# Attention of a two-layer block: un-normalised weights are transposed, 1/sum goes in with the gate, rotary products come before the turn

## The chip, the cores and the metric

The kernel runs on one core of a Trainium2 chip. The metric is the device time of one execution in microseconds, as the median of several runs. A profile of one execution gives the rows that are shown here. Engines in the rows: PE is TensorE (matmul), PEld its weight loads, DVE VectorE, ACT ScalarE, POOL GpSimd, SP the engine that issues the weight transfers.

## The reference

The reference is a long chain on one sequence of 256 positions, width 1024, in 32-bit floats: a first block (four mixers and a SwiGLU layer, then the mixers and a mixture of experts), and a second block of two layers. The change is in the second block.

- Even layer: a state-space scan beside a dilated attention. 24 heads of 64 in three groups of windows; queries and keys are normalised per head and get a partial rotary embedding; the three groups are merged by a softmax over their log-sums, so for one query the 512 weights of three groups are one softmax. The result is multiplied by silu(g), joined with the scan's output and projected.
- Odd layer: attention with 16 heads of 64. With 256 positions there is one block of keys, so it is causal softmax attention. Queries and keys are normalised and rotated the same way, the result is multiplied by silu(g) and projected:

```
q = partial_rope(rms_norm(q, q_norm), pos);  k = partial_rope(rms_norm(k, k_norm), pos)
p = softmax(masked(q @ k.T * scale));        o = (p @ v) * silu(g);        x = x + o @ w_out
```

## The kernel before

Features lie on partitions, positions along the free dimension (T = 256). Weights stream from HBM in pieces of up to 1 MB into a ring of six slots. ScalarE rounds each piece to a high part (`rounds`), VectorE or GpSimd subtracts to a low part (`rests`, `rest_piece`, L501), and TensorE takes each projection as three matmuls per tile (`mm3`). These matmuls, the bulk, fill most of the program. A matmul on full 32-bit floats (`mm`, L383) shows as two instructions in the trace.

Each engine runs its own program in a fixed order, written by hand: a string of letters (`EVEN`, `ODD`) that `walk` goes through, the same on every engine. A `.` is a step of the bulk (in these stretches half a piece, 24 matmuls), `Q` a step of the rotary turn, `A` of the attention, `R` of its reciprocals, `O` of the output projection, `D` of the scan, `Y` of splitting its output. Semaphores join the engines. The core of the odd layer is five times `AQRQ.`; that of the even one is `AQRQ` twice and `AQRQQ` twice, without bulk.

The rotary turn works on tiles of 128 features (two heads) by 256 positions, 24 in the even layer and 16 in the odd. It is x cos + (P x) sin, with a permutation P of features within a head (constant `pp`). The even layer's tiles come as three of queries, then three of keys; the odd layer's in turn. Step s on the engines:

- TensorE, `turn_pe`: for a key tile it spreads that tile's normalising factors over a bank ("key factors", eight instructions), then multiplies tile s - 1 by P into a bank of its own ("turn"), which must have been read for tile s - 2.
- VectorE, `turn_dve`: scales tile s ("unturned"; L399 for keys, L402 for queries), reads the turned tile s - 1 times sin (L2377, "sin part"), adds the cosine part (L2380, "turned").
- GpSimd, `turn_pool`: the tile times cos (L2391, "cos part"), and at three steps the low part of a weight piece.

The attention takes cases of two heads: eight in the even layer (128 queries by 512 keys and groups), eight in the odd (two query blocks, 384 columns). Three cases are under way at a time; in step t:

- TensorE, `attend_pe`: scores of case t; weights of case t - 1 turned so that keys lie on partitions, a matmul of each 128 by 128 block with a diagonal of 1/sum; values of case t - 2.
- VectorE, `attend_dve`: scales and masks the scores (L399), takes their bound (L2456), multiplies the values of case t - 2 by half the gate ("attended"), and in `R` takes the reciprocal of the sums (L2473).
- ScalarE, `attend_act`: the exponential with its sum (L411), the copy of the turned weights out of PSUM ("weights by key", L408), and in `R` the diagonals, identity times 1/sum (L408).

VectorE evacuates the scores of case t ahead of everything else in that step, since its queue is in order.

## Time and profile before

| | |
|---|---|
| median of 3 runs | 1939.07 us (1939.01 to 1939.71) |
| span of the profiled execution | 1942.9 us; the profile has no other time of it |
| PE busy | 1882.1 us, 97% |
| DVE busy | 1310.0 us, 67% |
| ACT busy | 943.8 us, 49% |
| POOL busy | 124.2 us, 6% |
| mean granted TensorE clock | 0.993 |

Matmuls are pipelined and their ends are modelled, so busy time of PE counts also what overlaps. A wait is put down to the engine and line whose semaphore came last. The granted clock is a share of 2.4 GHz.

### The profile page before, as it was taken

What the parts mean: (1) busy time and instruction counts of PE and PEld (TensorE: products, weight loads), DVE (VectorE), ACT (ScalarE), POOL (GpSimd) and SP (SyncE); (2) the same over time, 40 slices, a digit from 0 to 9 for tenths busy, and PEclk for the clock granted to TensorE, in tenths of its full rate; (3) what the DMA queues carried; (4) which work ended last, traced back from release to release, by engine and by line L of the source; (5) the groups of instructions that cost most, each with busy time, mean ns of one, the idle gap of its engine ahead of it and who ended that gap; (6) DMA issues with size and microseconds to landing.
All of it is one profiled execution on the core that took longest, in us unless ns stands there. A gap on an engine that the chain in (4) does not pass through costs nothing.

```text
span 1942.9 us, 34150 instructions
## 1 busy us (share of the span) xinstructions
PE 1882.1 (97%) x14477; PEld 1737.7 (89%) x14477; DVE 1310.0 (67%) x1864; ACT 943.8 (49%) x1150; POOL 124.2 (6%) x82
## 2 busy tenths in 40 slices
PE   9999999999999999999999999999999999889998
PEld 9889999999988999998888888888899989789978
DVE  7975566654599647665556668989888456856563
ACT  5353345434444423444435457767756453445453
POOL 0000000000000000000100011010200001100034
PEclk9999999999999999999999999999999999999999
DMA  8221246455542223544545568999945333314320
GB/s 309 88 88 56 100 165 224 163 185 184 182 140 88 72 63 134 197 171 158 182 153 194 182 229 312 331 328 335 334 180 173 131 109 119 111 54 164 131 88 23
DMA packets 52679, 321.84 MB, mean 166 GB/s; under 512 B 6320, under 2 KB 9648, under 8 KB 19760
## 3 DMA queue, kind: packets, MB, share of 16 engines
q1 hardware_dynamic: 52096, 317.76, 46.5%
q8 instruction: 115, 1.88, 0.4%
q10 hardware_dynamic: 432, 1.90, 0.3%
q14 instruction: 36, 0.29, 0.1%
HBM read 317.01 MB, written 1.05 MB: 164 GB/s over the span
## 4 chain that ended last, share of the span: by engine, by line
PE 78%; DVE 14%; ACT 4%; issue 3%; POOL 0%; DVEq 0%; ACTq 0%; POOLq 0%
PE b L383 77%; DVE s_arena L399 5%; DVE s_ring_lo L501 3%; ACT s_wh L408 2%; PE b L2055 1%; DVE s_arena L1433 1%; DVE s_arena L2456 1%; DVE s_arena L402 0%; ACT s_arena L408 0%; ACT s_arena L405 0%; DVE s_arena L637 0%; DVE s_arena L2377 0%; DVE s_roots L399 0%; ACT s_arena L411 0%; POOL s_ring_lo L501 0%
## 5 line engine op out<-in xcount | busy, mean ns | idle before, releaser
L501 DVE TENSOR_TENSOR s_ring_lo<-s_ring,s_wh 128x2048 fp32r<-128x2048 f32 (+3 forms) x310 | 648.1, 2096 | 309.3 <-ACT s_wh L408 308.7
L408 ACT ACTIVATE s_wh<-s_ring 128x2048 fp32r<-128x2048 f32 (+3 forms) x332 | 574.1, 1732 | 253.2 <-PE b L383 249.2
L383 PE MATMUL b<-s_Hh,s_wh 128*128 128x256 f32 x1832 | 536.2, 293 | 9.2 <-DVE s_arena_r L2983 4.2
L383 PE MATMUL b<-s_Hl,s_wh 128*128 128x256 f32 x1832 | 521.6, 285 | 0.0
L383 PE MATMUL b<-s_Hh,s_ring_lo 128*128 128x256 f32 x1832 | 521.4, 285 | 0.0
L383 PEld LDWEIGHTS b<-s_Hh,s_wh 128*128 128x128 f32 x1832 | 354.5, 194 | 20.0 <-issue 10.2
L383 PEld LDWEIGHTS b<-s_Hl,s_wh 128*128 128x128 f32 x1832 | 354.8, 194 | 0.5
L383 PEld LDWEIGHTS b<-s_Hh,s_ring_lo 128*128 128x128 f32 x1832 | 354.4, 193 | 0.0
L383 PE MATMUL b<-s_wh,s_arena_r 128*128 128x512 f32 (+1 forms) x942 | 296.4, 384 | 4.5 <-DVE s_arena_r L2294 3.7
L383 PE MATMUL b<-s_arena_r,s_wh 128*128 128x256 f32 x1184 | 214.6, 282 | 4.7 <-DVE s_arena L399 1.7
L383 PEld LDWEIGHTS b<-s_wh,s_arena_r 128*128 128x128 f32 x942 | 176.0, 188 | 38.9 <-DVE s_arena_r L2294 4.9
L383 PE MATMUL b<-s_arena 64*64 64x64 f32 (+7 forms) x2440 | 196.8, 260 | 11.5 <-ACT s_arena L408 3.6
L383 PEld LDWEIGHTS b<-s_arena 64*64 64x64 f32 (+3 forms) x2440 | 157.8, 149 | 42.0 <-issue 6.1
L408 ACT ACTIVATE s_arena<-b 128x256 f32<-128x256 f32 (+6 forms) x185 | 82.9, 476 | 229.4 <-PE b L383 204.1
L383 PEld LDWEIGHTS b<-s_arena_r,s_wh 128*128 128x128 f32 x1184 | 181.9, 188 | 7.0 <-DVE s_arena L399 3.1
L383 PE MATMUL b<-s_ring_lo,s_arena_r 128*128 128x512 f32 (+1 forms) x482 | 183.7, 381 | 0.0
L383 PE MATMUL b<-s_wh,s_Hh 128*128 128x256 f32 (+2 forms) x512 | 176.6, 345 | 0.0
L383 PE MATMUL b<-s_ring_lo,s_Hh 128*128 128x256 f32 (+2 forms) x512 | 170.4, 333 | 0.0
L383 PE MATMUL b<-s_arena_r,s_ring_lo 128*128 128x256 f32 x592 | 166.4, 281 | 0.0
L383 PE MATMUL b<-s_wh,s_Hl 128*128 128x256 f32 (+2 forms) x464 | 152.4, 329 | 0.0
L501 POOL TENSOR_TENSOR s_ring_lo<-s_ring,s_wh 128x1536 fp32r<-128x1536 f32 (+1 forms) x22 | 85.6, 3892 | 747.9 <-ACT s_wh L408 747.7
L383 PEld LDWEIGHTS b<-s_arena_r,s_ring_lo 128*128 128x128 f32 x592 | 111.3, 188 | 0.0
(195 smaller groups left out, 1925.1 us busy)
## 6 DMA issues: line engine op xcount, KB each, us to landing
s_ring<-fixed SPq DMA_DIRECT2D x158, 1024.0 KB, 4.9
s_ring<-experts SPq DMA_DIRECT2D x96, 1024.0 KB, 5.0
s_ring<-experts SPq DMA_DIRECT2D x48, 768.0 KB, 4.4
s_ring<-fixed SPq DMA_DIRECT2D x24, 256.0 KB, 4.1
s_c<-c SPq DMA_DIRECT2D x1, 1664.0 KB, 17.6
s_ring<-fixed SPq DMA_DIRECT2D x3, 512.0 KB, 5.9
s_arena<-s_arena SPq DMA_DIRECT2D x48, 32.0 KB, 1.9
s_c<-c ACTq DMA_DIRECT2D x1, 1344.0 KB, 6.1
```

What stands on the lines that cost most here:

```text
L383: return e.matmul(out, l, r, start=start, stop=True, skip_group_check=True)
L399: return e.scalar_tensor_tensor(out=out, in0=a, scalar=s, in1=b, op0=o0, op1=o1)
L408: return e.activation(out, x, ACT.Copy, scale=scale)
L501: e.tensor_tensor(l_, r_, h_.bitcast(F), SUB).then_inc(*up(engine, z % "lo", i))
L1433: e.tensor_tensor(Gm[o:o + 64, q // 2, 2 * h2:2 * h2 + 2, :], (b7, b6)[n % 2][o:o + 64, :].rearrange("p (a n) -> p a n", a=2), rwm, MUL).t ...
L2055: last = e.transpose(b[:, 128 * j:128 * j + n], m_vb[t % 2][0:n, 128 * j:128 * j + 128], ident[0:n, 0:n])
L2456: last = e.tensor_reduce(m[:, 0, hh, k:k + 1], v[:, at:at + n], AX.X, MIN)
```

## The change

In `turn_dve` the products with cos and sin are formed before TensorE's turn, on VectorE: for a query tile two instructions straight from the raw tile, for a key tile the scaled tile and then two products. TensorE turns the product with sin (the two halves that P exchanges have the same sin), and VectorE adds the turned tile, straight from PSUM, to the product with cos. The turn of a tile now waits until the tile before it has been added ("turned"). `turn_pool` is gone; GpSimd keeps the low parts of the late weight pieces in the odd layer.

In the attention the un-normalised weights are transposed (`e.transpose`, one instruction each) instead of multiplied with a diagonal, and the diagonals on ScalarE are gone. Before the values of a case TensorE spreads 1/sum over the free half of the bank, with one matmul per head and sum. VectorE first multiplies the gate by half of that and then the values by the result, two instructions that depend on each other.

```diff
@@ -2354,54 +2354,43 @@
                     spread(e, banks2[0], r, [tiles[s][0]]).then_inc(*up("PE", "key factors", name, s))
                 if s:
                     if s >= 2:
-                        e.wait_ge(*on("sin part", name, s - 2))
+                        e.wait_ge(*on("turned", name, s - 2))
                     mm(e, banks2[1][:, 0:T], c("pp"), tmps[s - 1][2], True).then_inc(*up("PE", "turn", name, s - 1))
...
         def turn_dve(e, name, tiles, banks2, tmps, raw):
+            cos, sin = {"even": (c("cpe"), c("spe")), "odd": (c("cp"), c("sp"))}[name]
             for s in range(len(tiles) + 1):
                 if s < len(tiles):
                     j, key, is_k = tiles[s]
-                    un = tmps[s][2]
+                    own, un, across = tmps[s]
                     if s >= 2:
-                        e.wait_ge(*on("turn", name, s - 2))
-                        e.wait_ge(*on("cos part", name, s - 2))
+                        e.wait_ge(*on("turned", name, s - 2))
                     if is_k:
                         e.wait_ge(*on("key factors", name, s))
-                        stt(e, un, raw[:, j, :], pc(key), banks2[0][:, 0:T], MUL, MUL).then_inc(*up("V", "unturned", name, s))
+                        stt(e, un, raw[:, j, :], pc(key), banks2[0][:, 0:T], MUL, MUL).then_inc(*up("V"))
+                        e.wait_ge(*now("V"))
+                        e.tensor_tensor(across, un, sin, MUL).then_inc(*up("V", "unturned", name, s))
+                        e.tensor_tensor(own, un, cos, MUL).then_inc(*up("V", "own part", name, s))
                     else:
-                        ts(e, un, raw[:, j, :], pc(key), None, MUL).then_inc(*up("V", "unturned", name, s))
+                        stt(e, across, raw[:, j, :], pc(key), sin, MUL, MUL).then_inc(*up("V", "unturned", name, s))
+                        stt(e, own, raw[:, j, :], pc(key), cos, MUL, MUL).then_inc(*up("V", "own part", name, s))
                 if s:
-                    tmp, tm2, un = tmps[s - 1]
                     e.wait_ge(*on("turn", name, s - 1))
-                    e.tensor_tensor(tm2, banks2[1][:, 0:T], c({"even": "spe", "odd": "sp"}[name]), MUL).then_inc(*up("V", "sin part", name, s - 1))
-                    e.wait_ge(*on("cos part", name, s - 1))
-                    e.wait_ge(*now("V"))
-                    e.tensor_tensor(raw[:, tiles[s - 1][0], :], tmp, tm2, ADD).then_inc(*up("V", "turned", name, s - 1))
-                yield
-
-        def turn_pool(e, name, tiles, tmps, pieces={}):
-            for s in range(len(tiles) + 1):
-                if s:
-                    tmp, tm2, un = tmps[s - 1]
-                    if s >= 3:
-                        e.wait_ge(*on("turned", name, s - 3))
-                    e.wait_ge(*on("unturned", name, s - 1))
-                    pool_free(e)
-                    e.tensor_tensor(tmp, un, c({"even": "cpe", "odd": "cp"}[name]), MUL).then_inc(*up("G", "cos part", name, s - 1))
-                if s in pieces:
-                    rest_piece(e, pieces[s], "G")
+                    e.wait_ge(*on("own part", name, s - 1))
+                    e.tensor_tensor(raw[:, tiles[s - 1][0], :], banks2[1][:, 0:T], tmps[s - 1][0], ADD).then_inc(*up("V", "turned", name, s - 1))
+                yield
...
@@ -2420,10 +2409,9 @@
                 if 1 <= t <= len(cases):
                     case = cases[t - 1]
                     for hh in range(2):
-                        e.wait_ge(*on("diagonal", name, t - 1, hh))
-                        for j, k in enumerate(case.blocks):
-                            last = mm(e, case.banks[hh][:, 128 * j:128 * j + 128], z.v[(t - 1) % 2][hh][:, 128 * j:128 * j + 128],
-                                      z.d[(t - 1) % 2][hh][k], True)
+                        e.wait_ge(*on("weights", name, t - 1, hh))
+                        for j in range(len(case.blocks)):
+                            last = e.transpose(case.banks[hh][:, 128 * j:128 * j + 128], z.v[(t - 1) % 2][hh][:, 128 * j:128 * j + 128], ident)
                         last.then_inc(*up("PE", "weights turned", name, t - 1, hh))
...
                     for hh in range(2):
                         e.wait_ge(*on("weights by key", name, t - 2, hh))
+                        e.wait_ge(*on("one over sum", name, t - 2, hh))
+                    for k in range(len(case.sums)):
+                        for hh in range(2):
+                            mm(e, case.banks[0][HALVES[hh], 256 + 128 * k:384 + 128 * k],
+                               z.m[t % 2][:, 2, hh, k:k + 1].broadcast_to([128, 64]), ident, True)
                     for n, (val, at, w_, to) in enumerate(case.vals):
                         for hh in range(2):
                             last = mm(e, case.banks[0][HALVES[hh], to:to + w_], val(hh), z.t[t % 2][hh][:, at:at + w_], n == 0)
...
                 if t >= 2:
                     case = cases[t - 2]
-                    o = case.banks[0][:, 0:max(to + w_ for _, _, w_, to in case.vals)]
+                    width = 128 * len(case.sums)
+                    o, over = case.banks[0][:, 0:width], case.banks[0][:, 256:256 + width]
+                    if case.gate.shape != o.shape:
+                        o, over = (z_.rearrange("p (a m) -> p a m", a=2) for z_ in (o, over))
+                    e.wait_ge(*on("out", li["og", (t - 2) // 2] if name == "oo" else li["eg", (t - 2) // 4]))
                     e.wait_ge(*on("values", name, t - 2))
-                    if case.gate.shape != o.shape:
-                        o = o.rearrange("p (a m) -> p a m", a=2)
-                    e.wait_ge(*on("out", li["og", (t - 2) // 2] if name == "oo" else li["eg", (t - 2) // 4]))
-                    stt(e, case.out, o, 0.5, case.gate, MUL, MUL).then_inc(*up("V", "attended", name, t - 2))
+                    stt(e, case.gate, over, 0.5, case.gate, MUL, MUL).then_inc(*up("V"))
+                    e.wait_ge(*now("V"))
+                    e.tensor_tensor(case.out, o, case.gate, MUL).then_inc(*up("V", "attended", name, t - 2))
...
                 if t < len(cases):
                     yield
-                    for hh in range(2):
-                        e.wait_ge(*on("one over sum", name, t, hh))
-                        if t >= 2:
-                            e.wait_ge(*on("weights turned", name, t - 2, hh))
-                        for k in range(len(cases[t].sums)):
-                            last = copy(e, z.d[t % 2][hh][k], ident, scale=z.m[t % 2][:, 2, hh, k:k + 1])
-                            last.then_inc(*(up("A", "diagonal", name, t, hh) if k == len(cases[t].sums) - 1 else up("A")))
...
                 last.then_inc(*(up("G", "tap pads") if z is e_pad[1] else up("G")))
-            e.wait_ge(c2_in, 16)
-            turn_pool(e, "even", e_tiles, e_tmps)
...
         def odd_pool(e):
-            turn_pool(e, "odd", o_tiles, o_tmps, {9: odd_late[0], 11: odd_late[1], 15: odd_late[2]})
-            for p in odd_late[3:]:
+            for p in odd_late:
                 rest_piece(e, p, "G")
```

## Rows read from the trace of the kernel before

**Rows 1.** Page, part 4: the chain that ended last, by engine.

```profile
PE 78%; DVE 14%; ACT 4%; issue 3%; POOL 0%; DVEq 0%; ACTq 0%; POOLq 0%
```

**Rows 2.** Window, length, busy PE, PEld, DVE, ACT, POOL (instructions); granted clock; DMA.

```profile
1664.00:1720.00 56.00, 45.63 (x406) 37.55 (x405) 49.04 (x123) 25.75 (x59) 8.71 (x12) 0.97 0.17 60
1862.00:1907.00 45.00, 39.90 (x330) 33.27 (x329) 31.51 (x89) 27.61 (x78) 20.47 (x12) 1.00 0.14 48
```

**Rows 3.** PE, two odd cycles: start, length, instructions [idle before <-releaser].

```profile
1871.88 3.26 PE L383 MATMUL b<-s_arena 64*128 64x128 f32 x28
1874.97 0.61 PE L383 MATMUL b<-s_c,s_roots 128*64 128x128 f32 x8
1875.50 0.70 PE L383 MATMUL b<-s_arena,s_c 128*128 128x256 f32 x2
1876.81 0.67 PE L383 MATMUL b<-s_arena,s_c 128*128 128x256 f32 x2 [0.61 <-DVE s_arena L2377]
...
1880.28 3.26 PE L383 MATMUL b<-s_arena 64*128 64x128 f32 x28
...
1886.10 0.67 PE L383 MATMUL b<-s_arena,s_c 128*128 128x256 f32 x2 [1.50 <-DVE s_arena L2377]
```

**Rows 4.** Timeline of DVE in the first of these cycles.

```profile
1875.45 0.42 DVE L399 SCALAR_TENSOR_TENSOR s_arena<-b,s_arena 128x256 f32<-128x256 f32 x1
1875.79 0.47 DVE L399 SCALAR_TENSOR_TENSOR s_arena<-s_arena,s_par,b 128x256 f32<-128x256 f32 x1
1876.24 0.42 DVE L2377 TENSOR_TENSOR s_arena<-b,s_c 128x256 f32<-128x256 f32 x1
1876.77 0.62 DVE L2380 TENSOR_TENSOR s_arena<-s_arena 128x256 f32<-128x256 f32 x1
```

**Rows 5.** Timeline of PE in an even cycle.

```profile
1690.88 0.67 PE L383 MATMUL b<-s_arena,s_c 128*128 128x256 f32 x2 [0.70 <-DVE s_arena L2377]
1693.11 4.16 PE L383 MATMUL b<-s_arena 64*128 64x256 f32 x44 [1.56 <-DVE s_arena L2380]
```

**Rows 6.** Timeline of DVE in the same even cycle.

```profile
1689.64 0.38 DVE L399 SCALAR_TENSOR_TENSOR s_arena<-b,s_arena 128x128 f32<-128x128 f32 x1
1689.92 0.47 DVE L399 SCALAR_TENSOR_TENSOR s_arena<-s_arena,s_par,b 128x256 f32<-128x256 f32 x1
...
1691.59 0.33 DVE L402 TENSOR_SCALAR s_arena<-s_arena,s_par 128x256 f32<-128x256 f32 x1
```

**Rows 7.** Timelines of PE: transposes, and weights turned by diagonals.

```profile
1514.19 0.64 PE L2725 MATMUL b<-s_c,s_arena 128*128 128x128 f32 x4
...
1672.58 2.05 PE L383 MATMUL b<-s_arena 128*128 128x128 f32 x16 [1.27 <-ACT s_arena L408]
```

**Rows 8.** L2380 (min, median, max); L399 with two SBUF inputs (count, busy, mean).

```profile
L2380 DVE TENSOR_TENSOR s_arena<-s_arena x40: 425/700/727, 1624.6 to 1905.0; 128x256 f32<-128x256 f32 x40
...
L399 DVE SCALAR_TENSOR_TENSOR s_arena<-s_arena 128x256 f32<-128x256 f32 x56 | 24.5, 475 | 2.1 <-ACT s_arena L2918 1.3
```

**Rows 9.** Timeline of PE at an earlier pair of rotary turns.

```profile
1844.79 0.67 PE L383 MATMUL b<-s_arena,s_c 128*128 128x256 f32 x2 [0.61 <-DVE s_arena L2377]
```

**Rows 10.** Timeline of PE at the last even cases.

```profile
1716.71 7.14 PE L383 MATMUL b<-s_arena 64*128 64x256 f32 x44 [2.36 <-ACT s_arena L408]
```

**Rows 11.** Short stretches, columns as in rows 2.

```profile
1688.80:1692.20 3.40, 2.04 (x18) 1.09 (x14) 3.26 (x10) 2.48 (x8) 0.87 (x2) 1.00 0.00 0
1712.70:1716.10 3.40, 1.65 (x22) 1.29 (x20) 3.05 (x9) 2.14 (x6) 0.00 (x0) 1.00 0.00 0
1716.10:1719.50 3.40, 2.79 (x15) 2.49 (x16) 1.37 (x4) 1.56 (x4) 0.00 (x0) 0.53 0.00 0
1784.30:1787.70 3.40, 3.40 (x30) 3.40 (x30) 2.29 (x2) 1.19 (x1) 0.00 (x0) 1.00 0.72 289
1791.10:1794.50 3.40, 3.40 (x18) 3.40 (x19) 1.75 (x1) 3.31 (x5) 0.00 (x0) 0.54 0.50 212
```

**Rows 12.** Timeline of POOL in the odd layer.

```profile
1870.41 4.64 POOL L501 TENSOR_TENSOR s_ring_lo<-s_ring,s_wh 128x2048 fp32r<-128x2048 f32 x1
```

More of the change, by code:

```diff
@@ L2399, in build @@
         Case = namedtuple("Case", "after banks parts sums blocks vals out gate part")
-        Buffers = namedtuple("Buffers", "v t d m")
+        Buffers = namedtuple("Buffers", "v t m")
         def attend_buffers(ar, n, groups):
             return Buffers([[ar(n) for _ in range(2)] for _ in range(2)], [[ar(n) for _ in range(2)] for _ in range(2)],
-                           [[[ar(128) for _ in range(groups)] for _ in range(2)] for _ in range(2)], [ar(3, 2, groups) for _ in range(2)])
+                           [ar(3, 2, groups) for _ in range(2)])
```

## The prediction

> **What bounds the kernel now.** I began with the chain of work that ended last: 78% of it is TensorE matmul, 14% VectorE [rows 1]. That is an average over a long program, so I went on to the busy time by stretch, for the two places the change touches: the even attention (1664 to 1720 us) and the odd one (1862 to 1907 us) [rows 2]. The reader is to see that they differ. In the even stretch VectorE is busy 49.0 of 56.0 us and TensorE 45.6: VectorE sets the pace. In the odd one TensorE is busy 39.9 of 45.0 us and VectorE 31.5: neither is full, so a few waits from one to the other cost 5 us.
>
> The order of TensorE's instructions shows where [rows 3]. An odd cycle is: the scores of a case, the weights turned (case before), the values (two before), key factors, a rotary turn, **a wait for L2377**, a second rotary turn, 24 projection matmuls, the next scores. The wait is 0.61 us in one cycle and 1.50 in the next. VectorE's order of the same moment [rows 4] shows what it waits for: after the scores VectorE evacuates them, gates the case two before (L399, 1875.45), multiplies out the next tile, and only then does the sine part (L2377) that frees the bank of the turn. The path is thus TensorE's scores, VectorE's whole row of work up to that release, TensorE's second turn, the projection. What stands between scores and second turn on TensorE itself is covered. The even cycle has the same form, with waits of 0.70 and 1.56 us [rows 5, 6].
>
> **The change on TensorE: less work, mostly not on the path.** A turned weight block is today a matmul with a diagonal, two instructions; 16 such instructions take 2.05 us. Four transposes elsewhere in the trace take 0.64 us [rows 7]. Both rows hold the full length of their last instruction; between them lie 12 instructions and 1.41 us, so 0.12 us each, if both kinds have one pace. A block then costs one instruction of 0.12 us and not two. The even layer has 8 cases of 8 blocks, the odd 8 of 6: 112 x 0.12 = -13.4 us. The matmuls that spread 1/sum are 4 instructions per even case and 8 per odd one; key factors, the same shape, take 0.61 us for 8 [rows 3], of which about 0.17 lies under what follows: 8 x 0.22 + 8 x 0.44 = +5.3 us. Net -8.1 us of TensorE time. Bounds for a transpose: 0.64 / 4 = 0.16 us, and no gain at all would be the 0.24 us of the pair it replaces. The Trainium skill (TensorE: Matmul & The Clock Gate, Terms) calls the transpose mode four times faster for FP32; the rows say twice, and by the page's figure some 6 us more would go, most of it from time that is covered.
>
> **The change on ScalarE and GpSimd.** 48 diagonal copies go (16 even cases' halves, 32 odd), and 40 cosine parts. Nothing on the path waits for them except the first even case (1.27 us, `ACT L408` [rows 7]); it is counted below. VectorE's adds (L2380) lose an odd delay: they take 700 ns by the median and 425 at least [rows 8], as most start while GpSimd's cosine part runs. The Trainium skill (SBUF — State Buffer, SBUF: two separate sides) says that GpSimd and a VectorE instruction with two SBUF inputs lock each other out; the two numbers agree with it.
>
> **The change on VectorE: this sets the time.** Steps are from start to start, since instructions overlap by some 0.08 us; a result that the next instruction needs costs a wait of 0.11 us instead (1876.24 + 0.42 to 1876.77) [rows 4].
> - Gating becomes two dependent instructions. Odd: today 0.34 us (1875.45 to 1875.79); after 0.42 + 0.11 + 0.34 = 0.87, **+0.53**. Even: today 0.28 (1689.64 to 1689.92) [rows 6]; after 0.38 + 0.11 + 0.28, **+0.48**.
> - Key tile, from its start to the release of the bank. Today 0.47 (with overlap 0.40) and 0.42: 0.82 us. After: 0.47 + 0.11, two multiplications of 0.34, the add 0.42 = 1.68, as the turn now waits for "turned" and both products stand ahead of that add in VectorE's queue: **+0.86**. Where VectorE today waits for the turn itself (0.45 instead of 0.40) [rows 4], +0.81.
> - Where VectorE is full, a tile counts in all. Query tile: today 0.25 (0.33 less the overlap [rows 6]) + 0.53 + 0.62 (0.70 less the overlap) = 1.40 us; after, two instructions with two SBUF inputs, 475 ns each [rows 8] less the overlap, and the add, 0.39 + 0.39 + 0.34 = 1.12: **-0.28**. Key tile: 0.40 + 0.53 + 0.62 = 1.55 today, 0.58 + 3 x 0.34 = 1.60 after, +0.05.
>
> Odd layer. Five cycles: three with the long wait +1.39, two with the short one +1.34: +6.9 us. Two earlier pairs of turns, the later at 1844.8 with a wait of 0.61 us [rows 9], get +0.85 each: +1.7. What TensorE saves inside the cycles only lengthens its wait. Outside them one case's transposes run in the open, -0.7, of which a later wait may eat half: -0.4. The last two transposed cases save 1.4 us, three spreads take 1.4 back. Sum **+8.2 us**.
>
> Even layer. Ahead of case 2 two query tiles shorten VectorE's row: -0.5. Cases 2 and 3: two gatings +0.96, three key tiles +0.15, one query tile -0.28: +0.8. Cases 4 and 5: two gatings +0.96, two query tiles -0.5, two key tiles +0.1, and the last pair, where the products delay the turn's release by 0.87 but the separate sine part goes (-0.53 behind it): +0.9. After case 6 TensorE waits 2.36 us for ScalarE's copies [rows 10]; that chain is unchanged. Behind it TensorE is the bound: eight instructions fewer in each of two cases, at 0.24 us each in the first, which runs at the lower clock (44 matmuls in 7.14 us [rows 10], against 4.16 [rows 5]), -1.9, and -1.0 in the second; three spreads +0.8; the later gating before the output projection +0.5: -1.6. Sum **-0.4 us**.
>
> **TensorE's clock.** Rows of it are clear, the effect is not. From 1712.7 to 1716.1 us TensorE was busy 1.65 of 3.40 us, and in the stretch behind it the granted clock was 0.53, the lower level, 1.2 GHz; from 1688.8, busy 2.04 of 3.40, it stayed at 2.4 GHz [rows 11]. In the changed kernel the wait before the second turn grows, by VectorE's delay and TensorE's own saving (0.3 us), from 0.61 to 2.2 us and from 1.50 to 3.1 in the odd cycles, from 0.70 to about 2.8 in the even ones. These are as long as the 2.36 us ahead of that fall. A price: at the lower clock 18 matmuls ran in 3.40 us, at the full one 30 [rows 11]; 12 x 0.12 = 1.4 us lost. Bounds: no fall, 0; one in each of the five odd cycles twice as long as this row, 14 us. I take three or four more stretches of 3.4 us than before, **+5 us**, by the nearest row, the wait of 2.36 us.
>
> Sum: 8.2 - 0.4 + 5 = +12.8 us. It is made against the profiled span of 1942.9 us, which lies 3.8 us above the median of the runs; 1939.1 + 12.8 = **1951.9 us**.
>
> **Rivals.** 0.2% of this kernel is 3.9 us, about what a measurement can tell from no change.
> - *The path grows, the clock stays.* Same steps, no more time at 1.2 GHz. For it: waits of 1.50 and 1.56 us left the clock alone. 1939.1 + 7.8 = 1946.9 us. Chance 0.20.
> - *The clock falls in nearly every cycle.* In this kernel it would do so if transposes counted for less than the matmuls that they replace: 7.8 + 14 = +21.8, 1960.9 us. The trace has four transposes at a time among matmuls, never a dozen beside a wait, so it speaks neither way. Chance 0.08. The Trainium skill (TensorE: Matmul & The Clock Gate, PE-mode transpose) says that transposes don't count as busy for the clock in the same way; no row here shows it.
> - *Other side: TensorE is the bound after all.* If VectorE had slack enough to release the bank before TensorE came to the second turn, TensorE's -8.1 us would all count: 1931 us. It decides if VectorE could release the bank 1.4 us sooner than it does; both waits in [rows 3] end at VectorE, against it. Chance 0.06.
> - *Nothing shows.* VectorE's additions and TensorE's savings cancel, because my delay of the release is half as large: within 3.9 us of 1939.1. Chance 0.06.
> - *GpSimd's splits of weights in the way.* They take 4.6 us each [rows 12], and nothing ties them to the rotary steps any more. A product with two SBUF inputs that starts under one would be held up as the adds are under the cosine parts [rows 8], here by up to 4.6 us, half of it for a typical hit: with one or two hits 1954 to 1957. The splits follow ScalarE's roundings, which end ahead of VectorE's evacuation of scores from PSUM, against it. Chance 0.05.
>
> My own case has 0.55, with its own range 1948 to 1960. Sum of the slower cases 0.55 + 0.20 + 0.08 + 0.05 = 0.88; faster 0.06; same 0.06. The range 1944 to 1961 leaves out the faster case, nearly all of "nothing", and part of the clock's worst.
>
> **What the new profile would show.** L2377's separate sine part and all of GpSimd's L2391 gone; VectorE busier by 8 gatings per layer; in the odd layer TensorE's wait before the second turn of 2 to 3 us, ended by the add; the cycle from scores to scores 9.7 us or more, where it was 8.4 (1871.88 to 1880.28 [rows 3]); transposes 0.11 us apart; more stretches at the lower clock in both attentions. I am wrong if those waits are still near 0.6 and 1.5 us, or if the clock keeps to 1.0 through the odd layer.

## The result, and the profile of the changed kernel

The changed kernel takes **1955.57 us** (median of 4 runs, 1951.31 to 1956.51) against 1939.39 us for the kernel before, run beside it (4 runs, 1939.01 to 1940.15). The ratio is 1.0071, 95% interval [1.0056, 1.0086]: slower by 16.2 us between the medians and by 13.8 us (10.9 to 16.7) by the ratio. A median of 1951.9 us was forecast.

The chain and the busy time of the two attentions in the changed kernel (columns as in [rows 2]); they answer to [rows 1, 2]:

```profile
PE 76%; DVE 15%; ACT 4%; issue 4%; POOL 0%; DVEq 0%; ACTq 0%; POOLq 0%
1664.00:1722.00 58.00, 44.41 (x373) 35.10 (x371) 49.13 (x132) 20.55 (x44) 0.00 (x0) 0.88 0.13 46
1862.00:1919.00 57.00, 44.31 (x331) 37.19 (x330) 33.02 (x98) 21.83 (x58) 14.32 (x4) 0.85 0.11 38
```

ScalarE has lost work and GpSimd keeps only its splits of weights; VectorE's busy time has hardly grown. TensorE is busy 44.4 and 44.3 us where it was 45.6 and 39.9, in the odd layer for the same number of instructions: the granted clock, 0.97 and 1.00 before, is now 0.88 and 0.85 (1.00 is 2.4 GHz, the lower level 1.2 GHz shows as 0.50). The windows are of different length because the stretches are: from the scores of case 2 to those of case 7 the odd layer took 44.1 us and now takes 57.2.

One odd cycle and the turn of the next on TensorE, which answer to [rows 3]:

```profile
1878.13 1.19 PE L383 MATMUL b<-s_arena,s_c 128*128 128x256 f32 x2 [2.08 <-DVE s_arena L2469]
...
1883.07 0.93 PE L383 MATMUL b<-s_arena 64*128 64x128 f32 x8
1883.93 0.87 PE L2414 MATMUL b<-s_c,s_arena 128*128 128x128 f32 x6
1884.73 0.66 PE L383 MATMUL b<-s_c,s_arena 128*64 128x128 f32 x8
1885.22 0.82 PE L383 MATMUL b<-s_arena 128*64 128x256 f32 x8
1885.87 0.61 PE L383 MATMUL b<-s_c,s_roots 128*64 128x128 f32 x8
1886.41 0.70 PE L383 MATMUL b<-s_arena,s_c 128*128 128x256 f32 x2
1890.15 0.67 PE L383 MATMUL b<-s_arena,s_c 128*128 128x256 f32 x2 [3.04 <-DVE s_arena L2469]
```

The rows are: a second turn, (projection,) scores, six transposes (L2414), the spread of 1/sum, the values, key factors, a first turn, and the second turn, which now waits 2.08 us in one cycle and 3.04 in the next, where it waited 0.61 and 1.50. VectorE in the same cycle, which answers to [rows 4]:

```profile
1887.01 0.41 DVE L399 SCALAR_TENSOR_TENSOR s_arena<-b,s_arena 128x256 f32<-128x256 f32 x1
1887.46 0.42 DVE L2461 TENSOR_TENSOR s_arena<-b,s_arena 128x256 f32<-128x256 f32 x1
1887.80 0.68 DVE L2479 TENSOR_TENSOR s_arena_r<-s_arena,s_arena_r 128x512 fp32r<-128x512 f32 x1
1888.40 0.47 DVE L399 SCALAR_TENSOR_TENSOR s_arena<-s_arena,s_par,b 128x256 f32<-128x256 f32 x1
1888.91 0.42 DVE L2373 TENSOR_TENSOR s_arena<-s_arena,s_c 128x256 f32<-128x256 f32 x1
1889.25 0.41 DVE L2374 TENSOR_TENSOR s_arena<-s_arena,s_c 128x256 f32<-128x256 f32 x1
1889.58 0.42 DVE L2381 TENSOR_TENSOR s_arena<-b,s_arena 128x256 f32<-128x256 f32 x1
1889.92 0.22 DVE L2469 RECIPROCAL s_arena<-s_arena 128x2 f32<-128x2 f32 x2
```

Two gating steps take 0.79 us (1887.01 to 1887.80; 0.87 was costed). Then come the rest of the case before (L2479), the un-turned key tile, its sine product (L2373), its cosine product (L2374), and the add (L2381) that frees the bank: 0.51 + 0.34 + 0.33 and the add's own 0.42, 1.60 us where 1.68 was costed. Both are shorter at one place: a result that the next instruction needs costs 0.04 us here (1887.01 + 0.41 to 1887.46; 1888.40 + 0.47 to 1888.91), not the 0.11 that I took from [rows 4]. In that row two semaphores are waited for, and the trace of the kernel before has a semaphore instruction of 0.02 us of its own (L2379) between L2377 and L2380, 40 times; the new pairs have none. That this makes the difference fits all rows, but no run separates it. The view names the reciprocal (L2469) as the releaser, but 1890.15 is 0.15 us behind the add's end (1890.00); the reciprocal only overlaps it.

What the clock does behind such a wait (columns as in [rows 2]):

```profile
1888.00:1891.35 3.35, 1.20 (x8) 1.18 (x9) 3.25 (x10) 2.66 (x5) 0.55 (x1) 1.00 0.01 2
1891.60:1895.00 3.40, 3.40 (x18) 3.32 (x16) 0.00 (x0) 0.00 (x0) 3.40 (x1) 0.50 0.00 0
```

Ahead, TensorE is busy for 1.20 of 3.35 us; behind, it is full and passes 18 matmuls in 3.40 us at the lower level, the price of [rows 11]. The end of the even layer, the scores of its last case (case 7) and the first instruction of the output projection:

```profile
1719.52 1.15 PE L383 MATMUL b<-s_arena 64*128 64x256 f32 x12 [1.50 <-ACT s_arena L408]
1724.83 0.50 PE L383 MATMUL b<-s_arena_r,s_wh 128*128 128x256 f32 x2 [1.90 <-DVE s_arena L2469]
```

These lie 5.31 us apart; the same two places of the kernel before are shown with its second profile below.

### The profile page after: what moved, and what is told of

It reads as the page before. It is cut to its first block, busy times and chain, and to the rows that moved or that the text cites. A ratio compares the mean times of both kernels' runs of the same rounds, so it can differ in the third digit from the quotient of the medians.

```text
span 1954.7 us, 34001 instructions
## 1 busy us (share of the span) xinstructions
PE 1879.9 (96%) x14461; PEld 1733.1 (89%) x14461; DVE 1316.2 (67%) x1900; ACT 928.8 (48%) x1102; POOL 94.8 (5%) x42
## 3 DMA queue, kind: packets, MB, share of 16 engines
HBM read 317.01 MB, written 1.05 MB: 163 GB/s over the span
## 4 chain that ended last, share of the span: by engine, by line
PE 76%; DVE 15%; ACT 4%; issue 4%; POOL 0%; DVEq 0%; ACTq 0%; POOLq 0%
PE b L383 75%; DVE s_arena L399 6%; DVE s_ring_lo L501 4%; ACT s_wh L408 2%; PE b L2055 1%; DVE s_arena L2449 1%; DVE s_arena L1433 1%; ACT s_arena L405 0%; ACT s_arena L408 0%; DVE s_arena L637 0%; DVE s_arena L402 0%; DVE s_roots L399 0%; DVE s_arena L2381 0%; DVE s_arena L2374 0%; ACT s_arena L411 0%
## 5 line engine op out<-in xcount | busy, mean ns | idle before, releaser
L383 PE MATMUL b<-s_arena 64*64 64x64 f32 (+5 forms) x2216 | 168.6, 258 | 8.7 <-ACT s_arena L1302 3.3
L383 PEld LDWEIGHTS b<-s_arena 64*64 64x64 f32 (+3 forms) x2216 | 132.3, 145 | 34.6 <-issue 5.1
```

The costliest lines, as they stand in the source:

```text
L383: return e.matmul(out, l, r, start=start, stop=True, skip_group_check=True)
```

## The experiments

For all kernels I measured two lengths in the trace, in us, each from the start of one group of TensorE instructions to that of another: the even layer (scores of case 0 to the output projection) and the five odd cycles (scores of case 2 to scores of case 7). Beside each stands the time at the lower clock within it. The kernels are described below, in the order of the table. The first two rows are the two profiles of the kernel before.

```
kernel              median us  ratio [95%]              even   lower clk  5 odd cycles   lower clk
before, first        1939.4                            59.38     6.8        44.06          0
before, again                                          57.05     0          44.05          0
changed              1955.6    1.0071 [1.0056,1.0086]  61.71    13.7        57.17         17.1
attention alone      1947.5    1.0038 [1.0024,1.0052]  61.07    13.7        49.19          6.8
rotary alone         1951.1    1.0057 [1.0043,1.0070]  57.56     3.4        50.91          6.8
changed, filled      1950.1    1.0051 [1.0038,1.0065]  59.44     3.4        50.19          0
own bank             1948.4    1.0042 [1.0028,1.0056]  60.28    13.7        49.52          6.8
gating later         1952.2    1.0047 [1.0034,1.0060]  62.75    13.7        47.71          3.4
both edits           1942.3    0.9997 [0.9988,1.0005]  59.78    10.2        42.58          0
before, gating later 1943.7    1.0005 [0.9996,1.0013]  58.41     0          43.14          0
attention, g. later  1942.8    1.0012 [1.0003,1.0021]  62.36    17.1        42.47          0
both, filled         1941.7    1.0004 [0.9995,1.0013]  60.24     6.8        42.57          0
both, filled, silu   1947.8    1.0038 [1.0024,1.0052]  60.22     6.8        48.25          3.4
before, filled       1939.4    0.9995 [0.9986,1.0004]  57.02     0          44.04          0
```

The medians of the kernel before, run beside each group, were 1939.3 us (first four experiments), 1942.7 (next four) and 1941.4 (last four), so kernels of different groups are compared by their ratios.

**Attention alone.** The rotary steps are those of the kernel before (the edit in words):

```diff
-  turn_pe, turn_dve (products ahead of the turn), no turn_pool
+  turn_pe, turn_dve, turn_pool of the kernel before
```

> The attention part of the change alone (transposes, 1/sum spread, two-step gating), with the rotary turns of the kernel before. If VectorE's way to the release of the turn's bank sets the time: one gating more on it per odd cycle, 5 x 0.53 = +2.7 us, transposes in the open -0.4 us, even layer 4 x 0.48 - 1.6 = +0.3 us, and one or two more stretches at the lower clock (waits before the second turn near 1.5 and 2.4 us), +2: 1939.4 + 4.6 = 1944 us. If TensorE were the bound: its 8.1 us fewer show at once, 1931 us. If the clock falls because transposes count for little, whatever the waits: falls in nearly every odd cycle, 1939.4 + 2.6 + 14 = 1956 us. If the whole loss lies in the rotary part: 1939 us.

```profile
1884.56 0.67 PE L383 MATMUL b<-s_arena,s_c 128*128 128x256 f32 x2 [2.25 <-DVE s_arena L2377]
...
1894.84 0.67 PE L383 MATMUL b<-s_arena,s_c 128*128 128x256 f32 x2 [1.29 <-DVE s_arena L2377]
```

The waits grow by 0.68 and 0.75 us, to 1.29 and 2.25, a little less than the 1.5 and 2.4 expected; the five cycles by 5.1 us, of which two stretches of 3.4 us at the lower clock are 2.8 and the path 2.3 (2.7 expected). But the kernel lost nearly twice what I expected (8.2 us between the medians, not 4.6), and the table says where: 4.0 us in the even layer, not 0.3, with 13.7 us at the lower clock.

**Rotary alone.** The reverse (in words):

```diff
-  turn_pe, turn_dve, turn_pool of the kernel before
+  turn_pe, turn_dve of the changed kernel; attention as before
```

> The rotary part alone (products ahead of the turn, on VectorE; none on GpSimd), with the diagonal matmuls of the kernel before. If VectorE's way to the release sets the time: 5 cycles x 0.86 + two earlier pairs 1.7 = +6.0 us in the odd layer, about -0.4 us in the even one, the clock +2: 1947 us, with waits before the second turn near 1.4 and 2.3 us. If TensorE were the bound: nothing is taken from it, 1939 us. If transposes are what the clock punishes: the clock stays as before, 1945 us.

```profile
1886.95 0.77 PE L383 MATMUL b<-s_arena,s_c 128*128 128x256 f32 x2 [2.29 <-DVE s_arena L2462]
...
1897.58 0.67 PE L383 MATMUL b<-s_arena,s_c 128*128 128x256 f32 x2 [1.33 <-DVE s_arena L2462]
```

The waits are those expected (1.4 and 2.3). The five cycles grow by 6.9 us, 2.8 of it two stretches at the lower clock, 4.1 the path (4.3 expected). There is no transpose in this kernel, and its clock falls as often in the odd layer as in the one above: behind the waits of 2.3 us, in both. The whole lost 11.8 us between the medians, where 7.6 were expected. The profile shows 8.8 of it: the five cycles, 1.4 for the two earlier pairs (waits of 1.25 and 1.34 us where 0.61 stood) and 0.5 in the even layer; the rest is not located.

**The changed kernel with its waits filled.** Idle matmuls go ahead of each long wait in front of a turn, and nothing else is changed:

```diff
+ if s in FILL:                        # odd: 8:8, 10:7, 12:11, 14:7, 16:11
+     e.wait_ge(*on("out", ...))       # even: 16:8, 18:7, 20:5, 23:5, 24:3
+     fill(e, free_bank[:, 256:384], FILL[s])
  if s:
      e.wait_ge(*on("unturned", name, s - 1))
```

> The changed kernel, with 3 to 11 idle matmuls (128 columns, into a bank that nobody reads) put into each of TensorE's waits before the second turn of a cycle: five in the odd layer, five in the even one; VectorE's work is untouched. If the path sets about half of the loss and the lower clock the rest: the path stays (odd cycles 9.8 and 10.7 us or so), the granted clock is 1.0 in both attentions but perhaps for the wait for ScalarE's copies near 1716 us, and 13.6 + 17 us at the lower clock go, worth some 7 us: 1948 us. If the path is the whole loss and the clock costs nothing, or if the matmuls delay TensorE itself: 1955 us or more. If the clock is the whole loss: 1940 us. If transposes pull the clock down: the clock still falls behind them.

The two attentions by window (columns as in [rows 2]), and under them TensorE's timeline in the same odd cycle as above:

```profile
1664.00:1720.00 56.00, 45.59 (x428) 38.23 (x428) 49.79 (x132) 21.15 (x45) 0.00 (x0) 0.99 0.15 54
1862.00:1913.00 51.00, 48.12 (x428) 41.92 (x428) 32.96 (x98) 21.83 (x58) 13.34 (x4) 1.00 0.12 43
```

```profile
1885.94 2.62 PE L383 MATMUL b<-s_c 128*128 128x128 f32 x22
1889.14 0.67 PE L383 MATMUL b<-s_arena,s_c 128*128 128x256 f32 x2 [0.59 <-DVE s_arena L2473]
```

The second turn still comes 3.0 us behind the end of the first (1886.10 to 1889.14; 1887.11 to 1890.15 above); only what lies in between is work now, and the clock stays at 1.00. The five cycles go from 57.17 to 50.19 us: **7.0 us of the loss was the clock**, 17.1 us of it at the lower level, 1.4 per stretch of 3.4. The 6.1 us above the kernel before (44.06) are the path alone. By the medians the filling gives back 5.5 us, by the ratios 3.9. The wait for ScalarE's copies ahead of case 7 of the even layer was not filled, and the one fall that is left stands behind it:

```profile
1717.89 1.15 PE L383 MATMUL b<-s_arena 64*128 64x256 f32 x12 [3.10 <-ACT s_arena L408]
1723.91 0.51 PE L383 MATMUL b<-s_arena_r,s_wh 128*128 128x256 f32 x2 [0.99 <-DVE s_arena L2465]
```

From these scores to the output projection it is 6.02 us, in the changed kernel, which has the full clock at this place, 5.31: this fall costs 0.7 us.

**A key tile turned in the bank of its factors.** That bank is free as soon as the un-turned tile is formed, so the second turn waits neither for the cosine product nor for the add:

```diff
+ in_factors = lambda s: tiles[s][2] and not (s + 1 < len(tiles) and tiles[s + 1][2])
- if s >= 2: e.wait_ge(*on("turned", name, s - 2))
- mm(e, banks2[1][:, 0:T], ...)
+ # wait only for the last tile turned in the same bank
+ mm(e, banks2[0 if in_factors(s - 1) else 1][:, 0:T], ...)
```

> The changed kernel, with a key tile turned in the bank in which its factors were spread (free once the un-turned tile is formed), so that TensorE's second turn waits neither for the cosine product nor for the add of the tile before. If VectorE's way to the release sets the time: shorter by 0.34 + 0.42 us in each of the seven odd pairs, -5.3 us, waits near 1.3 and 2.3 us, with two or three falls of the clock fewer, -3: 1947 us. If TensorE or the clock alone were the cause, or if the second turn waits for something else: within 2 us of 1955.6.

```profile
1886.97 1.22 PE L383 MATMUL b<-s_arena,s_c 128*128 128x256 f32 x2 [2.28 <-DVE s_arena L2377]
...
1897.31 0.70 PE L383 MATMUL b<-s_arena,s_c 128*128 128x256 f32 x2 [1.32 <-DVE s_arena L2377]
```

Each wait is 0.76 us shorter than in the changed kernel (3.04 to 2.28, 2.08 to 1.32), which is the figure expected to the hundredth; three of the five stretches at the lower clock are gone with them. The median is 7.1 us lower, where 8.6 were expected.

**Gating moved behind the reciprocals.**

```diff
- (in the first part of a cycle) gating of case t - 2
+ (behind both e.reciprocal) gating of case t - 2
```

> The changed kernel, with both gating instructions moved on VectorE behind the reciprocals of the cycle, so that they stand no more between the scores and the release of the turn's bank. If VectorE's row of work up to the release sets the time: 0.87 us less in each of five odd cycles, -4.3 us, waits near 1.2 and 2.2 us, and two or three falls of the clock fewer, -3; 1955.6 - 7.3 = 1948 us. If the loss came from the length of VectorE's work in all, wherever it stands: no change, 1955 us. If the later gating delays the case after next instead: a new wait ahead of scores, and over 1955.

```profile
1879.49 0.67 PE L383 MATMUL b<-s_arena,s_c 128*128 128x256 f32 x2 [1.29 <-DVE s_arena L2475]
...
1889.24 0.67 PE L383 MATMUL b<-s_arena,s_c 128*128 128x256 f32 x2 [2.25 <-DVE s_arena L2475]
```

The waits become 1.29 and 2.25 us, 0.79 less each, and the five cycles 47.7 us (3.4 at the lower clock). The even layer is the longest of all: its output projection waits 2.96 us where it waited 1.90. From the scores of case 7 to that projection it is 6.37 us, not 5.31: what leaves the path in one layer is late in the other. The ratios of the two kernels differ by 4.7 us, where 7.3 were expected.

**Both edits.** The two diffs above together.

> The changed kernel with both edits: key tile turned in the bank of its factors, gating behind the reciprocals. If the path is as thought: each odd cycle is 0.76 + 0.87 us shorter than in the changed kernel (-8.2), two earlier pairs -1.5, and no wait is over 1.6 us, so that the clock's falls in the odd layer go (-5 to -6): 1940 us, level with the kernel before, or 1937 if TensorE's fewer matmuls show in the even layer too. If a wait of another kind takes over (ScalarE's copies, the silu evacuations): 1943 us or more.

```profile
1882.81 0.70 PE L383 MATMUL b<-s_arena,s_c 128*128 128x256 f32 x2 [1.49 <-DVE s_arena L2377]
...
1890.86 0.70 PE L383 MATMUL b<-s_arena,s_c 128*128 128x256 f32 x2 [0.53 <-DVE s_arena L2377]
```

The odd layer's loss is undone: waits of 0.53 and 1.49 us, no fall of the clock, and five cycles of 42.6 us, 1.5 less than before the change (0.6 less than in the kernel before with its gating later, the next one). The whole is level with the kernel before, 0.9997 [0.9988, 1.0005], since the even layer keeps 2.7 us of loss. Of this 1.1 us is the later gating itself, between the scores of case 7 and the output projection (6.37 us against 5.29).

**The kernel before with its gating moved, and the kernel before again.**

> The kernel before, with its one gating instruction moved behind the reciprocals: 0.34 us less on VectorE's way to the release in five odd cycles, -1.7 us, and up to -1 in the even layer where VectorE is the fuller engine only if a wait there ended at it: 1937.5 us. If the way to the release is not what sets the odd cycle: 1939.3.

The long cycles lose 0.33 us, the short ones nothing (8.41 us still, wait still 0.61 us): 0.9 us in five cycles, where 1.7 were expected. So the 0.61 us of a short cycle before the change is a floor: VectorE waits there for TensorE's key factors (0.19 us idle) and starts the sine part right at the end of the first turn. The even layer is 1.4 us longer, 1.1 of it ahead of the output projection (6.35 us from the scores of case 7): the gating now stands behind the reciprocals, one of which waits 0.81 us for ScalarE's exponential. The whole is not faster (1.0005), a miss.

> The kernel before, once more, unchanged, for a second profile: the first one's own time lay 3.8 us above the runs. If that came from stretches at the lower clock, this one shows fewer of them (the 6.8 us near 1716 or 1791 us halved or gone) and a span near 1938; the odd cycles keep 8.4 and 9.3 us.

Its span was 1938.9 us, 4.0 less than that of the first profile. The end of the even layer by window and on TensorE's timeline, the places of [rows 10, 11]:

```profile
1712.55:1715.95 3.40, 1.64 (x22) 1.27 (x20) 3.04 (x9) 2.15 (x6) 0.00 (x0) 1.00 0.00 0
1716.30:1719.70 3.40, 3.16 (x30) 2.95 (x32) 2.14 (x5) 1.19 (x4) 0.00 (x0) 1.00 0.00 0
```

```profile
1716.54 4.15 PE L383 MATMUL b<-s_arena 64*128 64x256 f32 x44 [2.36 <-ACT s_arena L408]
1721.83 0.50 PE L383 MATMUL b<-s_arena_r,s_wh 128*128 128x256 f32 x2 [1.13 <-DVE s_arena L2473]
```

The same wait of 2.36 us, with 1.64 of 3.40 us busy (1.65 in the first profile), and this time the clock does not fall: 44 matmuls take 4.15 us, not 7.14. Whether a wait of this length brings the clock down differs from execution to execution of one program.

**Attention alone with the gating later.**

> The attention part of the change alone, with both gating instructions behind the reciprocals; rotary turns as before. If only VectorE's way to the release counts: against the attention part alone (8.2 us above the kernel before), 0.87 us less in each of five odd cycles, -4.3, and the two falls of the clock in the odd layer go, -2.5: 1.4 us above the kernel before run beside it, from falls in the even layer. If the transposes are worth having by themselves once the gating is out of the way: below the kernel before. If two gatings cost wherever they stand: 5 us above or more.

```profile
1884.79 0.67 PE L383 MATMUL b<-s_arena,s_c 128*128 128x256 f32 x2 [1.46 <-DVE s_arena L2377]
...
1892.89 0.67 PE L383 MATMUL b<-s_arena,s_c 128*128 128x256 f32 x2 [0.61 <-DVE s_arena L2377]
```

The five odd cycles are 1.6 us shorter than before the change (42.47 against 44.06), at the full clock. Moving the gating gave 0.9 us of that by itself (43.14), so the transposes are worth 0.7 us there. The even layer loses 5.3 us against 57.05, with 17.1 us at the lower clock, and the ratio, 1.0012, stays above one.

**Both edits with the even layer's waits filled**, and **the same with the silu evacuation later** (a 0.69 us instruction of VectorE):

```diff
+ even layer only: {16: 7, 18: 4, 23: 3, 24: 3} idle matmuls ahead of turns
+ and {4: 7, 7: 12} ahead of the scores of cases 4 and 7
  VectorE's order in the odd layer, for the last of the two:
- "AQRQ." "AQRQ." "AQRQ." "AQRQ." "AQRQ."
+ "AQRQ." "AQRQ" "AQ.RQ." "AQRQ" "AQ.RQ."
```

> Both edits, and idle matmuls in TensorE's six longest waits of the even layer (4 to 12 each, ahead of second turns and of scores, into a free bank). If the odd layer of this version is 2.6 us shorter than before's and the even layer loses its gain to one to three stretches at the lower clock: those go, 3 us under the version without them, and 3 us or more under the kernel before. If the falls have another cause, or the matmuls get in the way: level with the kernel before.

The expected 3 us did not come (1.0004). The even layer has 6.8 us at the lower clock, not 10.2, but elsewhere: the fall near 1699 stands behind a wait of 1.78 us that I had not filled, and another stretch of 3.4 us begins just behind the layer's end. The layer is no shorter (60.24 us against 59.78). The stretch that the filling took away at its end had cost nothing: from the scores of case 7 to the output projection it is 6.37 us with it and without it, as VectorE sets the pace there.

> As the last one, with VectorE's evacuation of the odd layer's gate projections (0.69 us, ahead of the scores' evacuation in every second cycle) moved behind the key tile's products in the two cycles with waits of 1.5 us. If that evacuation is why those cycles are 1 us longer: 1.3 us less in all. If the turn there waits for something else, or the weights' remainders that move with it come late: no gain, or a loss.

VectorE's, GpSimd's and TensorE's timeline in the first cycle with the silu evacuation moved:

```profile
1885.92 5.16 DVE L399 SCALAR_TENSOR_TENSOR s_arena<-s_arena,s_par,s_c 128x256 f32<-128x256 f32 x2
```

```profile
1886.09 4.71 POOL L501 TENSOR_TENSOR s_ring_lo<-s_ring,s_wh 128x2048 fp32r<-128x2048 f32 x1 [11.56 <-ACT s_wh L408]
```

```profile
1883.88 0.70 PE L383 MATMUL b<-s_arena,s_c 128*128 128x256 f32 x2 [1.13 <-DVE s_arena L2381]
1885.14 0.38 PE L383 MATMUL b<-s_Hh,s_wh 128*128 128x256 f32 x1 [0.56 <-DVE s_arena L399]
...
1891.47 0.71 PE L383 MATMUL b<-s_arena 64*128 64x128 f32 x6 [3.20 <-DVE s_arena L2389]
```

A miss that teaches more than it cost. The turn's wait falls from 1.49 to 1.13 us, and the projection then waits 0.56 us for the bank that the silu evacuation frees. But the 3.7 us that this cycle lost (12.75 against 9.02) come from the first row: the two query products, 0.86 us elsewhere, took 5.16, as GpSimd's split (second row) had begun 0.2 us ahead of the second of them. The add that the next scores need stood behind it. Here is the rival of GpSimd's splits: against the kernel with both edits filled, the products came 0.2 us later in the cycle and the split 0.4 us earlier, and the two met.

**The kernel before, filled** with 5 and 8 idle matmuls ahead of the scores of cases 4 and 7:

> The kernel before, with 5 and 8 idle matmuls in its two longest waits of the even layer, ahead of the scores of cases 4 and 7 (1.56 and 2.36 us). If part of the spread of its runs (1939.1 to 1944.7) is a fall of the clock behind the wait of 2.36 us that comes in some executions and not in others: a median 1 to 2 us under that of the kernel before, and a smaller spread. If not: no change.

Its 11 runs lie between 1938.8 and 1941.7 us, those of the kernel before beside it (27) between 1938.7 and 1944.4. The medians are 2.1 us apart, which is what was expected, but the ratio, 0.9995 [0.9986, 1.0004], does not exclude one.

## Why the prediction was right, and where its terms were off

The second profile of the kernel before (span 1938.9 us) has no fall of the clock in either attention and is the better basis. Against it the changed kernel's span is 15.8 us longer: even layer +4.7, from there to case 2 of the odd layer -0.1, the five odd cycles +13.1, the rest -0.3; the -1.7 ahead of the even layer had arisen before the first instruction that the change touches (-1.8 at 1617 us).

- **Mechanism.** Right: VectorE's row of work up to the release of the turn's bank sets the odd cycle. Waits forecast at 2.2 and 3.1 us measured 2.08 and 3.04. Own bank and later gating take off 0.76 and 0.79 us per wait, and together undo the odd layer's loss.
- **Five odd cycles, path.** +6.9 forecast, +6.1 measured with the waits filled (cycles of 9.57 and 10.55 us against 8.40 and 9.29, so +1.17 and +1.26 where 1.34 and 1.39 stood). The difference is the dependence that I costed at 0.11 us, twice in each cycle, and that takes 0.04: some 0.15 us, which leaves 1.19 and 1.24. The first of the three cycles that I counted as long had a wait of 0.89 us before, not 1.50; it grew by 1.26 all the same.
- **Earlier pairs.** +1.7 forecast; waits of 1.25 and 1.34 us where 0.61 stood, +1.4. From case 1 to case 2, where the transposes run in the open, -1.05 and not -0.4: no later wait ate half of it.
- **Even layer, path.** -0.4 forecast. With the waits filled it is 59.44 us, and 58.7 without the 0.7 us of the stretch at the lower clock that is left, against 57.05: **about +1.7**. In parts: up to the scores of case 2 -0.65 (12.24 us for 12.89), cases 2 and 3 +1.1, cases 4 and 5 +1.2, from case 6 on 0.0, where -0.5, +0.8, +0.9 and -1.6 stood. The last term failed: behind case 6 TensorE is not the bound. The scores of case 7 come 6.51 us behind those of case 6 in both kernels, with a wait for ScalarE's copies of 3.10 us where it was 2.36, and the output projection 5.31 us behind them where it was 5.29, with a wait for VectorE of 1.90 us where it was 1.13. TensorE's saving turned into waiting. Its larger part was also reckoned at the lower clock of a fall that the second profile does not have. The 1.27 us that the first even case waited for its diagonals, "counted below", stand in no term of the sum. The stretch from case 1 to case 2 became 1.17 us shorter and the one before it 0.52 longer; rotary alone, which keeps the diagonals, has nearly the same (-1.07 and +0.52), attention alone -0.47 and 0, so the gain lies mostly in the rotary steps. (The +0.48 of an even gating is +0.49 by its own terms.)
- **Clock.** +5 forecast for three or four more stretches. Here is the step that was mis-sized: 30.8 us at the lower clock in both attentions, nine stretches. They cost 7.0 us in the odd cycles and 3.0 in the even layer (61.71 less 58.7), less there per stretch, since VectorE sets the pace and covers part. The price of 1.4 us per stretch in the odd layer was exact; the number of them was not. The forecast counted from the first profile, which had two stretches of its own in the even layer (59.38 against 57.05 us, 2.3 us): against it there are seven more, and 7.7 us.
- **The sum.** The path is 8.1 us longer in all where 7.8 was forecast; that this agrees so well is luck, since the odd part was 1.7 us too high (6.5 for 8.2) and the even part 2.1 too low. What is over the forecast is the clock. Path and clock together are 18.1 us; the span shows 15.8, since the changed kernel's profile was 1.7 us ahead before the change begins and gains 0.6 in the parts around the odd cycles.
- **The rivals.** *Nothing shows*: excluded by the interval. *The path grows, the clock stays*: excluded by the windows at 0.88 and 0.85. *The clock falls in nearly every cycle*: in four of five, but one stretch each, two behind the last, so 7.0 us and not the 14 of this rival. Its ground, that transposes count for less, is not needed in the odd layer: there the kernel with no transposes falls as often as the one with no rotary change, and those with transposes and waits of 1.5 us at most (both edits; attention, gating later) do not fall at all. The Trainium skill (TensorE: Matmul & The Clock Gate, PE-mode transpose) says that transpose mode doesn't count as busy in the same way; the odd layer neither needs nor excludes it. In the even layer every kernel with transposes and unfilled waits has 10 to 17 us at the lower clock, and those with diagonals 0 to 6.8; but their waits are longer too, by what TensorE saves, and no run here separates the two. It stays open. *TensorE the bound*: excluded, attention alone is slower. *GpSimd's splits*: in the changed kernel no product took more than 0.43 us (L2373, L2374) or, with the factor, 0.49; the split nearest to them began 0.4 us behind the start of both:

```profile
1890.05 0.86 DVE L399 SCALAR_TENSOR_TENSOR s_arena<-s_arena,s_par,s_c 128x256 f32<-128x256 f32 x2
```

```profile
1890.80 4.56 POOL L501 TENSOR_TENSOR s_ring_lo<-s_ring,s_wh 128x2048 fp32r<-128x2048 f32 x1 [16.43 <-ACT s_wh L408]
```

In the run with the silu evacuation moved it happened, at 4.3 us for one hit: the mechanism and its price (up to 4.6 us) were right, and the changed kernel misses it by 0.4 us. The Trainium skill (SBUF — State Buffer, SBUF: two separate sides) describes this as a lock that whichever starts first holds for its whole instruction; the trace of that run agrees for the second product, which ends at 1891.1, the split at 1890.8. That the split in turn waited for the first product, then under way, shows at most in part in its row (4.71 us, 4.55 for the next split).

**What is left of a better version.** None beats the kernel before beyond the interval. Both edits gain 1.5 us in the odd layer and give it back in the even one, where VectorE is the fuller engine, fewer matmuls only mean longer waits, and the later gating costs 1.1 us at the end. No run moves the gating in the odd layer alone; by these rows I estimate 1 us less, about what the interval of one comparison hides.

## What to carry to other kernels

Before taking work from TensorE, look which engine's result ends its waits: here an estimated 8 us less of TensorE's work bought 1 us, where it ran in the open between case 1 and case 2 of the odd layer, and little else, while 1.2 us more of VectorE's work ahead of a release cost it 1.2 us in each cycle, and as much again when the longer wait brought the clock down. A wait that grows from 1.5 to 2 or 3 us, as here, is to be priced twice, once as itself and once as the slower work behind it; a handful of idle matmuls in it is a cheap test of which part is which. And where an operation is made to wait for a buffer, look first for another that is free sooner: the bank of the key factors took 0.76 us out of each wait, and no row shows a cost of it.

## What the runs showed of the hardware that I had not expected

- The same wait of 2.36 us, with 1.64 and 1.65 of 3.40 us busy ahead, was followed by 0.53 of the full clock in one execution and by 1.00 in another of one and the same program. The spread of this kernel's times, 1938.7 to 1944.7 us, goes with the clock: of the 27 executions beside the last group, the seven under 1939.6 us had a mean granted clock of 0.996, the three over 1944.3 us one of 0.993.
- In the five odd cycles a single wait of up to 1.69 us never brought the clock down; those of 2.08 to 3.04 us mostly did (not the first of the changed kernel, 2.44 us, nor the first of 2.25 us with the gating later). The kernel with the silu evacuation moved, whose waits of 1.13 and 0.56 us stand close together, had one fall behind such a pair.
- A VectorE product that began 0.2 us behind a GpSimd instruction on SBUF took 4.8 us, and 0.48 us elsewhere.
- A stretch at the lower clock cost 1.4 us in the odd layer, 0.7 us at the end of the even one, and nothing there once VectorE's gating stood later (6.37 us with the fall and without it).
- Transposes of 128x128 fp32 tiles follow each other every 0.11 us (a group of eight takes 1.09 us, one of six 0.87). The eight diagonal matmuls that they replace, 16 instructions, took 2.05 us: about half, as the four transposes of [rows 7] had said.
